# Output product of a hybrid attention and pooling step: pieces of 384, 384 and 256 columns in place of 512 and 512

## The reference

```
h     = LN(x) * (1 + scale) + shift                 # scale, shift, gate from the conditioning c
proj  = h @ w_in                                    # q, k, v, gates, pooling input
mixed = [attention(q, k, v) * silu(g_attn), pool(u) * silu(g_pool)]
y     = mixed @ w_out                               # 1152 x 1024 times 1024 x 1024
out   = LN(alpha * x + gate * y) * ln_g + ln_b
```

## Time and profile before

| | us |
|---|---|
| three runs | 444.65, 443.43, 444.64 |
| median | 444.64 |
| profiled execution: its own time | 444.71 |
| span from first to last instruction in it | 442.9 |
| PE busy / PEld busy / DVE busy | 424.0 / 367.9 / 276.8 |

### The profile page before, as it was taken

How to read it: one execution, slowest core, us unless ns; L and a number is a source line. 1 busy time by engine, 2 the same in 40 slices (tenths; PEclk the granted TensorE clock), 3 DMA queues, 4 the chain that set the end, 5 groups by cost and what they waited for, 6 DMA issues and landing times.

```text
span 442.9 us, 6736 instructions
## 1 busy us (share of the span) xinstructions
PE 424.0 (96%) x2604; PEld 367.9 (83%) x2604; DVE 276.8 (62%) x538; ACT 123.3 (28%) x305; POOL 126.2 (28%) x103
## 2 busy tenths in 40 slices
PE   4699989999999999999999999999999999999993
PEld 1366979898999999998799898899987878888883
DVE  6355685321126666647666663785886987888875
ACT  3453542202110001443343352433471110000000
POOL 2436662012223211265232222421002233333300
PEclk9889999999999999999999999999999999999998
DMA  8999600505500511111200120101483121222231
GB/s 294 419 419 381 242 1 1 209 30 182 193 32 18 147 47 49 35 26 47 55 2 6 49 54 6 49 7 49 85 270 117 53 99 53 93 95 96 95 141 50
DMA packets 23687, 47.59 MB, mean 107 GB/s; under 512 B 12068, under 2 KB 14500, under 8 KB 22344
## 3 DMA queue, kind: packets, MB, share of 16 engines
q1 hardware_dynamic: 23656, 47.16, 30.7%
HBM read 41.71 MB, written 6.36 MB: 109 GB/s over the span
## 4 chain that ended last, share of the span: by engine, by line
PE 91%; DVE 2%; DMA 2%; issue 1%; SPq 1%; ACT 1%; POOL 1%; DVEq 0%
PE proj_ps L665 15%; PE proj_ps L666 15%; PE proj_ps L667 15%; PE proj_ps L802 8%; PE proj_ps L804 8%; PE proj_ps L803 8%; PE s_ps L701 3%; PE s_ps L560 3%; DMA wada<-w_ada 2%; PE t_ps L730 2%; PE proj_ps L655 2%; PE proj_ps L616 2%; PE proj_ps L629 2%; PE t_ps L589 2%; PE proj_ps L617 1%
## 5 line engine op out<-in xcount | busy, mean ns | idle before, releaser
L665 PE MATMUL proj_ps<-h_hi,w_hi 128*128 128x384 f32 x384 | 134.2, 349 | 0.0
L667 PE MATMUL proj_ps<-h_hi,w_lo 128*128 128x384 f32 x384 | 129.1, 336 | 0.0
L666 PE MATMUL proj_ps<-h_lo,w_hi 128*128 128x384 f32 x384 | 129.1, 336 | 0.0
L1359 POOL TENSOR_TENSOR w_lo<-w_raw,w_hi 128x1024 fp32r<-128x1024 f32 x16 | 39.9, 2494 | 145.9 <-ACT w_hi L919 145.9
L665 PEld LDWEIGHTS proj_ps<-h_hi,w_hi 128*128 128x128 f32 x384 | 72.2, 188 | 4.0 <-issue 1.3
L666 PEld LDWEIGHTS proj_ps<-h_lo,w_hi 128*128 128x128 f32 x384 | 72.3, 188 | 0.8
L667 PEld LDWEIGHTS proj_ps<-h_hi,w_lo 128*128 128x128 f32 x384 | 72.2, 188 | 0.0
L802 PE MATMUL proj_ps<-wo_hi,m_hi 128*128 128x512 f32 (+1 forms) x152 | 58.8, 387 | 0.4 <-DVE mixed L1148 0.4
L804 PE MATMUL proj_ps<-wo_hi,m_lo 128*128 128x512 f32 (+1 forms) x152 | 58.4, 384 | 0.0
L803 PE MATMUL proj_ps<-wo_lo,m_hi 128*128 128x512 f32 (+1 forms) x152 | 58.4, 384 | 0.0
L1143 DVE SCALAR_TENSOR_TENSOR mixed<-th,proj_ps 128x384 f32<-128x384 f32 x24 | 13.3, 552 | 47.1 <-ACT th L933 47.1
(11 more groups left out here) (174 smaller groups left out, 631.4 us busy)
## 6 DMA issues: line engine op xcount, KB each, us to landing
w_raw<-w_in SPq DMA_DIRECT2D x18, 512.0 KB, 4.9
wada<-w_ada SPq DMA_DIRECT2D x8, 1024.0 KB, 18.1
xs<-x_all SPq DMA_DIRECT2D x9, 512.0 KB, 11.6
xf<-x_all SPq DMA_DIRECT2D x9, 512.0 KB, 4.0
wada_late<-w_ada SPq DMA_DIRECT2D x2, 2048.0 KB, 8.2
y_out<-yr SPq DMA_DIRECT2D x8, 512.0 KB, 2.9
wo_raw<-w_out SPq DMA_DIRECT2D x4, 512.0 KB, 3.3
wo_rest<-w_out SPq DMA_DIRECT2D x4, 512.0 KB, 8.5
```

Of the source, the lines that this page charges most:

```text
L665: pe.matmul(bank[:, 0:CW], w_hi[:, w, k, :], hi, start=(k == 0), stop=False)
L666: pe.matmul(bank[:, 0:CW], w_hi[:, w, k, :], lo, start=False, stop=False)
L667: mm = pe.matmul(bank[:, 0:CW], w_lo[:, w, k, :], hi, start=False, stop=(k == KT - 1))
L1359: pool.tensor_tensor(w_lo[:, b % 2], w_raw[:, b % RAW], w_hi[:, b % 2].bitcast(F32), ALU.subtract).then_inc(wlo_done, 1)
```

## The change

The pieces become 384, 384 and 256 columns for each tile; the last tile has 384, 384, 128 and 128. There are 28 pieces in place of 19. Waits that counted two pieces a tile count `len(PIECES)`. Statistics still cover blocks of 512 columns (so none after a tile's first piece, one after its second, one after its third), and blocks of 128 on the last tile, for which `bnst` is larger. `SLOTS` is not edited: it names pieces by their number, and the numbers now stand for other columns. Lines behind the edits are one higher than before (L802 is L803, and so on).

```diff
-OUTPUTS = [(t, 512 * half, 512) for t in range(TILES) for half in range(2)]
-OUTPUTS[-1:] = [(TILES - 1, 512, 256), (TILES - 1, 768, 256)]
+PIECES = ((0, 384), (384, 384), (768, 256))
+OUTPUTS = [(t, w0, n) for t in range(TILES) for w0, n in PIECES]
+OUTPUTS[-1:] = [(TILES - 1, 768, 128), (TILES - 1, 896, 128)]
...
-    bnst = place("bnst", [P, 2, 24])
+    bnst = place("bnst", [P, 2, 48])
...
-                    sp.wait_ge(r_done, 2 * (t - 1))
+                    sp.wait_ge(r_done, len(PIECES) * (t - 1))
...
-                    act.wait_ge(y_done, 2 * (t - 1))
+                    act.wait_ge(y_done, len(PIECES) * (t - 1))
...
-            for m in range(2 * TILES):
-                if m % 2 == 0 and 2 <= m // 2 + 1 < TILES:
-                    mixed_high(m // 2 + 1)
+            for m in range(len(OUTPUTS)):
+                if OUTPUTS[m][1] == 0 and 2 <= OUTPUTS[m][0] + 1 < TILES:
+                    mixed_high(OUTPUTS[m][0] + 1)
...
-                size = 512 if t < TILES - 1 else 256
+                size = 512 if t < TILES - 1 else 128
```

## The result

Ten runs of each kernel: 444.06 us in the median before, 446.93 with the change. The ratio of the runs is 1.0077, with a 95% interval from 1.0057 to 1.0097. The change makes the kernel slower by 2.9 us or 0.6% by the medians, and by 3.4 us by the ratio; 447.5 had been forecast.

The account below looks back on a forecast made before the run. PE, busy 96% of the span, was taken to bound the kernel. The terms -0.8 + 2.6 - 0.3 + 0.9 + 0.4 gave +2.8 us on the median of 444.64, so 447.5 us, range 444.8 to 448.7.

Parts of the forecast that it names:

- Tiles 0 to 7: Output product of the first eight tiles: 384, 384, 256 columns take 0.4638 us in place of 0.4680; -0.8 us.
- The last tile: Last tile's product: 48 matmuls of 128 columns bound by weight loads at 0.115 us each; +2.6 us.
- The row of 9-column matmuls: Profile row of eight 9-column matmuls with 128 x 128 loads, 0.115 us each, taken as the price at 128 columns.
- The tail: DVE's work after the last matmul: shorter instructions on 128 columns save 0.4, the larger join costs 0.1; -0.3 us.
- Slice 6: Tile 0: PE reaches slice 6 at 337.5, before DVE's low part is ready at 338.41; PE waits 0.9 us.
- Slot 22: Second half of slot 22 needs step 19's copy, at 354.4; PE waits 0.4 us, ends 0 and 1.0.
- Costs at nothing: DVE's extra 0.4 us a tile is covered by idle time, banks free in time, other waits and increments cost nothing.
- The first rival: Narrow pieces go by their columns, not loads: 444.9 us with the waits (chance 0.14), 443.5 without (0.06).
- The second: Rival: 384 columns in the output product go at its rate, 0.1757 us a matmul; +3.6 us, 448.2; chance 0.18.

Follow-up runs that it names:

- last_as_before: Changed kernel with the last tile cut into 512, 256 and 256 columns as before; ratio 1.0003 to the kernel before.
- half_load: Changed kernel with 64 of 128 tokens stationary in the last tile's two 128-column pieces; ratio 1.0017 to the kernel before.
- pool_later: Changed kernel with POOL starting the low part of tile 1's m only after all low parts of w_out; ratio 1.0014 to the kernel before.
- first_as_before: Changed kernel with tile 0 cut into 512 and 512 columns as before; ratio 1.0041 to the kernel before.
- widths run: Changed kernel with tiles 2 to 7 cut into other widths, 64 to 480 columns; executed once, 0.108 us a matmul at 64 columns, 0.1867 at 416.

## Why the prediction was right

Forecast +2.8 us, measured +2.9. By its steps:

- *Tiles 0 to 7*, forecast -0.8 at 0.10 a tile: 0.07 a tile, -0.5. The price of 384 was right at 0.1733. That of 256 was a little off: 24 matmuls of it are what is left of 11.17 us, 11.17 - 48 x 0.1733 = 2.85, or 0.1188 each, where two pieces of 256 in a row had 0.1172.
- *The last tile*, forecast +2.6: +2.4. The row of 9-column matmuls gave 0.115 for what took 0.110, because the first of its eight distances, 0.14, held the change from another kind of work. That the loads bind was the step on which the sign hung; last_as_before and half_load bear it out.
- *The tail*, forecast -0.3: -0.3.
- *Slice 6*, forecast 0.9: 0.8 in the list of waits, and 1.15 on the path. The ends of the two streams gave the 0.9 rightly; PE's 0.15 us behind the semaphore and the short wait at slice 7, 0.1, were left out. pool_later and first_as_before take it away by two ways, at 1.2 to 1.4 us together with slot 22's.
- *Slot 22*, forecast 0.4 from ends of 0 and 1.0: 0.2.
- *Costs at nothing* held: in the tiles from 2 on the pieces follow one another at 0.1733 and 0.1188 with no gap, so no wait for a bank.

The mechanism of each step is there, and so is its sign. That the sum is right to 0.1 us is luck in part: the gain was 0.3 too great and slice 6 0.25 too small, and the last tile and slot 22 were 0.2 too great each.

One reading behind the gain was wrong: that a cost per matmul, whatever its width, doesn't show. It does in the widths run, as 13 ns on top of the columns from 288 to 416. Columns of 256 and 512 hid it because theirs differ, 10 to 12 ns and 21. In these terms two matmuls of 512 carried 2 x 20.7 = 41.4 ns on top, and the three in their place carry 13.3 + 13.3 + 12.1 = 38.7. That is 2.7 ns less, and times 24 about the 0.07 us a tile.

The first rival (narrow pieces by their columns) is refuted by 0.110 at 128 and by 0.108 at 64 columns. The second (384 at this stage's rate) did not occur in the changed kernel. One tile of the widths run had its price, though not for its reason.

## What to carry to other kernels

Matmuls that load 128 columns of float32r weights each took 0.108 to 0.112 us here, whether 64 or 224 columns streamed past. Cutting the moving side to 128 columns to shorten the tail took 0.3 us off it and put 2.4 on the stream. Before speeding up the engine that sets the time, look for what it reaches sooner: here a margin of 1.3 us in the timeline turned into a loss of 1.15, and the cause (DVE and POOL holding each other up) had been hidden in the kernel before. The cheaper width gained only when the narrow pieces and the waits that came with it were gone: 0.7 us of 112.

## What the runs showed of the hardware that I had not expected

At a granted clock of 1.00, float32r matmuls with a load each cost their columns at 2.4 GHz plus 13 ns from 288 to 416 columns, and plus 21 at 512, not in proportion to the width; between them 448 had 14 once and 20 once, 480 had 17 once and 20 once. The same width can settle at one of two prices for a whole piece (384 at 0.1733 or 0.1767, 448 at 0.2004 or 0.2067), 384 with the same columns of `w_out`; the cause is open. Under 64-column loads the 128-column stream went at 0.060 us.
